# One high-weight product of 512 columns for both parts of h in the projection of an SSD recurrence, with the halves of the bank added on VectorE

## The chip, the cores and the metric

The kernel runs on one core of one Trainium2 chip. The metric is the device time of one execution in microseconds (us). Before the change three runs gave 1707.39, 1708.99 and 1709.05 us, median 1708.99. The profiled execution took 1709.76 us, of which the profile's span covers 1708.0 us.

## The reference

One decoder layer on x of 2048 tokens by 1024 features, all float32. `h` is a normalised and modulated x; `proj = h @ w_in` is split among a gated linear attention group (GLA) and a Mamba-2 group (SSD); both results are joined, multiplied by `w_out`, normalised and added to x. The change lies in the SSD part, cut here to what it computes:

```
z, xbc, dt_raw = parts of h @ w_in
xbc = silu(causal_depthwise_conv(xbc, conv_w, conv_b))      # 4 taps per channel, plus a bias
xs, B, C = split(xbc)
dt = softplus(dt_raw + dt_bias);  A = -exp(a_log)
y = ssd_chunked(xs, dt, A, B, C)     # h_t = exp(dt_t A) h_{t-1} + dt_t B_t x_t^T, y_t = C_t h_t
y = y + d_skip * xs;  y = rms_norm(y * silu(z)) per group
```

Every product with a weight is made to nearly full float32 precision out of three products: with w = w_hi + w_lo and h = h_hi + h_lo (hi is the part that the fast format keeps, lo the rest), w·h is taken as w_hi·h_hi + w_hi·h_lo + w_lo·h_hi.

## The kernel before, in words

The kernel has three stages: `front` (norms, GLA, most of the projection), `ssd` (the SSD recurrence with its own part of the projection) and `project_out`. The change touches `ssd` alone, which begins at about 786 us of the span.

`ssd` goes over 2 groups of heads, and in each over 8 blocks of 256 tokens: 16 **steps**. A step projects the block n in eight **units** and, between them, works off the recurrence of the block before, n-1, in two **tiles** of 128 tokens:

- Units 0 to 5 (`u < UZ`) are convolved channels. A unit is 8 slices of the contraction (KT) times 3 products (PASSES), so 24 matmuls with a weight slice of 128x128 as the stationary operand and 256 token columns moving (L1805). All accumulate in the left half of one bank of PSUM, `ps[:, PROJ + u % 2, 0:B2]`.
- Units 6 and 7 are the gate z: 24 matmuls of 512 columns each (L1809).

Each engine goes through the units in an order written out by hand, and a unit waits for the one two before it to have left its bank (`unit_out`).

- **PE** (`tensor`): tile_in of tile 0 (transposes, L1833 and L1836, and one product, L1837); units 0, 1; tile_out of tile 0 (L1845, L1852, L1857); tile_in of tile 1; units 2, 3; tile_out of tile 1; units 4, 5; turn of tile 0 (L1865); units 6, 7; turn of tile 1.
- **ACT** (`scalar`): evacuates each unit. For units 0 to 5 that is a copy of the bank's left half to `before` (L1550) and, of the same columns, times the last tap plus the bias, to `acc` (L1552). Between them stand the high parts of the next h (L1542), the squares (L1576) and normed rows (L1583) of both tiles, one SiLU over all six units (L1562), then after unit 6 the table load and exponentials of `decays` (L1567, L1568), which wait for `seg_ready`, the evacuation of z (L1557) and the rows y (L1593).
- **DVE** (`vector`): tile_in (L1704 to L1713), the three other taps of each unit (L1684, three instructions, each waiting for the one before by `conv_step`), the low parts of h (L1668), tile_out (L1724, L1727, L1731, L1735), the history of three columns (L1697) and last the 16 instructions of `segments` (L1745), behind which `seg_ready` comes.
- **POOL** (`gpsimd`): per tile `ends` (L1473), `decay_state` (L1480) and `skip` (L1488); after both tiles the small steps to 1/rms (L1494, L1497) and y_diff (L1509).
- **SP** and the DMA queues load h, weights and store y; the change does not touch them.

The waits that matter below: PE's product L1852 waits for DVE's L1713 (`wt_ready`); PE's turn L1865 waits for ACT's L1583 (`yn_ready`), that one for POOL's L1497, which stands on POOL behind `skip` of tile 1, which waits for DVE's L1724 of tile 1. `seg_ready` leads to ACT's exponentials, behind which ACT evacuates z and then unit 0 of the next step.

Of the kernel before, what the change touches and what calls it, by code (L numbers as in the profile page):

```python
# [21 lines left out]
ALU = mybir.AluOpType  # L22
ACT = mybir.ActivationFunctionType

P = 128
HI, LO = 0, 1

PASSES = ((HI, HI), (HI, LO), (LO, HI))
# [3 lines left out]
def wait(eng, sem, count):  # L32

    if not isinstance(count, int) or count > 0:
        eng.wait_ge(sem, count)
# [1262 lines left out]
def ssd(nc, sems, y_stored, unit_done, h_ready, xd_ready, w_rows, w_sum_d, conv_col, convb_col, d_row, norm_col, ps, ident, tok, w, w_raw, hl_all, halves, w_even,  # L1298
        h_d, ac_d, y_d, column, T, KT, G, HG, GW, XT, NS, SP_, INNER, VAL, TAPS, B2, TB2):

    UB, UC, UX, UZ = 0, 1, 2, 2 + XT
    UCONV, U = UZ, UZ + XT
# [3 lines left out]
    HIST = TAPS - 1  # L1306

    PROJ, X, BC, Y, YI, ST, YT = 0, 2, 3, 4, 5, 6, 7
# [5 lines left out]
    with ExitStack() as ctx:  # L1314
        def sb(name, shape, dt=F32):
            return ctx.enter_context(nc.sbuf_tensor(name, shape, dt))

        def sem(name):
            return sems.enter_context(nc.semaphore(name))

        hl = hl_all[:, 0].rearrange("p k c n -> p (k c n)").rearrange("p (q k c n) -> p q k c n", q=2, k=KT, c=2)
# [3 lines left out]
        before = sb("c_before", [P, UCONV, HIST + B2])  # L1325
        acc = sb("c_acc", [P, UCONV, B2])
# [29 lines left out]
        conv_step = sem("c_conv_step"); conv_ready = sem("c_conv_ready")  # L1356
# [20 lines left out]
        def order(g, u):  # L1377

            return u - UZ if g == 0 else g * U - UZ + u
# [5 lines left out]
        def channel(g, u):  # L1385

            return INNER // P + (u - UB) * G + g if u < UX else g * XT + u - UX
# [128 lines left out]
        def scalar(act):  # L1516
# [27 lines left out]
            def evacuate(n, g, u, par):  # L1544
                act.wait_ge(unit_done, n * UP + u + 1)
                if u < UCONV:

                    wait(act, hist_ready, n)
                    ch = channel(g, u)
                    act.activation(before[:, u, HIST:], ps[:, PROJ + u % 2, 0:B2], ACT.Copy)  # L1550
                    wait(act, xbc_ready, n)
                    act.activation(acc[:, u, :], ps[:, PROJ + u % 2, 0:B2], ACT.Identity,  # L1552
                                   scale=conv_col[:, HIST, ch:ch + 1], bias=convb_col[:, ch:ch + 1]
                                   ).then_inc(unit_out, 1)
                else:
                    wait(act, gated_ready, (n - 1) * TB2)
                    act.activation(z[:, par, u - UZ, :], ps[:, PROJ + u % 2, :], ACT.Silu).then_inc(unit_out, 1)  # L1557
# [91 lines left out]
        def vector(dve):  # L1649
# [29 lines left out]
            def convolve(n, g, u):  # L1679

                dve.wait_ge(unit_out, n * UP + u + 1)
                ch = channel(g, u)
                for k in range(HIST):
                    op = dve.scalar_tensor_tensor(out=acc[:, u, :], in0=before[:, u, k:k + B2],  # L1684
                                                  scalar=conv_col[:, k, ch:ch + 1], in1=acc[:, u, :],
                                                  op0=ALU.mult, op1=ALU.add)
                    if k < HIST - 1:
                        op.then_inc(conv_step, 1)
                        dve.wait_ge(conv_step, (n * UCONV + u) * (HIST - 1) + k + 1)
                op.then_inc(conv_ready, 1)  # L1690

            def history(n, s_last):
# [100 lines left out]
        def tensor(pe):  # L1793

            def unit(n, g, u, par):

                if g > 0 or u >= UZ:
                    pe.wait_ge(w_ready, order(g, u if u < UZ else U - 1) + 1)
                wait(pe, unit_out, n * UP + u - 1)
                for k in range(KT):  # L1800
                    if u == 0 and k % QK == 0 and not (isinstance(n, int) and n < 2):
                        pe.wait_ge(h_ready, (n - 2) * QS + k // QK + 1)
                    for i, (a, b) in enumerate(PASSES):
                        if u < UZ:
                            mm = pe.matmul(ps[:, PROJ + u % 2, 0:B2], w[:, u, k, a, :], hl[:, par, k, b, :],  # L1805
                                           start=(k == 0 and i == 0), stop=(k == KT - 1 and i == 2))
                        else:
                            t = u - UZ
                            mm = pe.matmul(ps[:, PROJ + u % 2, :], hl[:, par, k, a, t * P:(t + 1) * P],  # L1809
                                           w_z[:, k, b, :], start=(k == 0 and i == 0),  # L1810
                                           stop=(k == KT - 1 and i == 2))
                mm.then_inc(unit_done, 1)
# [402 lines left out]
```

## Time and profile before

| | before |
|---|---|
| median of 3 runs | 1708.99 us |
| profiled execution, its span | 1709.76 us, 1708.0 us |
| PE busy (matmuls) | 1625.9 us, 95% |
| weight loads busy | 1400.2 us, 82% |
| DVE busy | 1053.3 us, 62% |
| ACT busy | 841.4 us, 49% |
| POOL busy | 388.7 us, 23% |
| L1805, 2304 matmuls of 256 columns | 295.3 us busy |
| L1684, 288 instructions of the taps | 161.5 us busy |
| L1550 and L1552, 96 each | 36.9 and 53.9 us busy |

How to read it: busy shares are of the whole span, over three stages with different limits. A matmul's own duration overlaps that of the next one, so the pace of a run of matmuls is read from the starts of two groups in the timeline and not from a mean duration. "Idle before, releaser" names the instruction whose semaphore ended the wait; in the timeline a row with xN merges N instructions that follow each other on the line.

### The profile page before, as it was taken

What the parts mean: (1) busy time and instruction counts of PE and PEld (TensorE: products, weight loads), DVE (VectorE), ACT (ScalarE), POOL (GpSimd) and SP (SyncE); (2) the same over time, 40 slices, a digit from 0 to 9 for tenths busy, and PEclk for the clock granted to TensorE, in tenths of its full rate; (3) what the DMA queues carried; (4) which work ended last, traced back from release to release, by engine and by line L of the source; (5) the groups of instructions that cost most, each with busy time, mean ns of one, the idle gap of its engine ahead of it and who ended that gap; (6) DMA issues with size and microseconds to landing.
All of it is one profiled execution on the core that took longest, in us unless ns stands there. A gap on an engine that the chain in (4) does not pass through costs nothing. (4 is left out here: it accounts for less than half of the span.)

```text
span 1708.0 us, 27489 instructions
## 1 busy us (share of the span) xinstructions
PE 1625.9 (95%) x10022; PEld 1400.2 (82%) x10022; DVE 1053.3 (62%) x1752; ACT 841.4 (49%) x1496; POOL 388.7 (23%) x449
## 2 busy tenths in 40 slices
PE   5899999999899999998999999999999999999996
PEld 5688888888788888877888887888888878888885
DVE  3543554465544554445677777876777754785986
ACT  5555555545544554453554545655544545234332
POOL 5000000110422222200232222222322220451421
PEclk9899999999999999998999999999999999999998
DMA  9423252255333533344132124322222226675885
GB/s 279 164 87 112 83 178 71 72 167 145 126 117 127 189 125 130 127 125 136 50 112 75 68 74 142 117 81 78 103 74 74 99 87 221 233 241 169 302 273 181
DMA packets 131359, 231.16 MB, mean 135 GB/s; under 512 B 9907, under 2 KB 81859, under 8 KB 126134
## 3 DMA queue, kind: packets, MB, share of 16 engines
q1 hardware_dynamic: 121830, 189.71, 34.6%
q10 hardware_dynamic: 8592, 39.85, 6.4%
q0 software_dynamic: 832, 0.22, 0.2%
q8 instruction: 63, 1.03, 0.2%
q14 instruction: 42, 0.34, 0.1%
HBM read 177.05 MB, written 52.70 MB: 135 GB/s over the span
## 5 line engine op out<-in xcount | busy, mean ns | idle before, releaser
L1131 PE MATMUL ps<-hl,w 128*128 128x512 f32 x1488 | 374.1, 400 | 0.1
L1131 PEld LDWEIGHTS ps<-hl,w 128*128 128x128 f32 x1488 | 274.9, 189 | 56.6 <-issue 1.4
L1805 PE MATMUL ps<-hl,w 128*128 128x256 f32 x2304 | 295.3, 288 | 5.0 <-PEq L302 5.0
L1805 PEld LDWEIGHTS ps<-hl,w 128*128 128x128 f32 x2304 | 283.1, 193 | 13.2 <-issue 13.1
L1137 PE MATMUL ps<-w,hl 128*128 128x256 f32 x1536 | 203.1, 289 | 3.8 <-DVE w L830 3.8
L1137 PEld LDWEIGHTS ps<-w,hl 128*128 128x128 f32 x1536 | 192.8, 193 | 6.5 <-DVE w L830 4.2
L1684 DVE SCALAR_TENSOR_TENSOR c_acc<-c_before,conv_col,c_acc 128x256 f32<-128x256 f32 x288 | 161.5, 562 | 46.5 <-ACT c_acc L1552 39.5
L1809 PE MATMUL ps<-hl 128*128 128x512 f32 x768 | 178.6, 391 | 0.0
L1809 PEld LDWEIGHTS ps<-hl 128*128 128x128 f32 x768 | 143.0, 188 | 29.3 <-DVE hl L1653 0.2
L2188 PE MATMUL ps<-w,hl 128*128 128x512 f32 x720 | 164.2, 389 | 0.4 <-DVE hl L2127 0.4
L2188 PEld LDWEIGHTS ps<-w,hl 128*128 128x128 f32 x720 | 135.0, 188 | 28.8 <-issue 0.8
L1550 ACT ACTIVATE c_before<-ps 128x256 f32<-128x256 f32 x96 | 36.9, 384 | 220.6 <-PE ps L1805 220.6
L454 POOL TENSOR_SCALAR mse<-ms 128x1 f32<-128x1 f32 x60 | 15.6, 260 | 567.1 <-ACT squares L629 567.1
L2188 PE MATMUL ps<-hl 128*128 128x512 f32 x576 | 131.0, 389 | 0.0
L2188 PEld LDWEIGHTS ps<-hl 128*128 128x128 f32 x576 | 108.1, 188 | 22.4
L819 DVE TENSOR_TENSOR hl<-x_sb,hl 128x1024 fp32r<-128x1024 f32 x48 | 60.1, 1253 | 57.5 <-ACT hl L613 57.4
L880 DVE SCALAR_TENSOR_TENSOR state<-state,dec,ps 128x256 f32<-128x256 f32 x56 | 26.9, 480 | 105.4 <-PE ps L1174 105.3
L830 DVE TENSOR_TENSOR w<-w_raw,w 128x1024 fp32r<-128x1024 f32 x30 | 37.4, 1251 | 55.3 <-ACT w L559 55.3
L1488 POOL TENSOR_TENSOR c_yi<-c_yi,c_xd 128x512 f32<-128x512 f32 x32 | 41.4, 1293 | 131.9 <-DVE c_yi L1724 131.9
L890 DVE SCALAR_TENSOR_TENSOR y<-ps,norm_col,gz 128x128 f32<-128x128 f32 x120 | 36.3, 343 | 56.8 <-PE ps L1182 33.2
L2147 DVE TENSOR_TENSOR d_mixed<-d_mixed,ps 128x512 f32<-128x512 f32 x64 | 42.4, 683 | 44.6 <-PE ps L2188 23.6
L1745 DVE SCALAR_TENSOR_TENSOR c_decay<-c_ac,tok,c_past 128x128 f32<-128x128 f32 x256 | 68.6, 345 | 0.0
(247 smaller groups left out, 2624.8 us busy)
## 6 DMA issues: line engine op xcount, KB each, us to landing
x_sb<-h SPq DMA_DIRECT2D x52, 512.0 KB, 3.9
w_raw<-in_w_in SPq DMA_DIRECT2D x42, 512.0 KB, 4.4
c_ac<-step_sums ACTq DMA_DIRECT2D x16, 1024.0 KB, 4.7
d_a_raw<-mixed_in SPq DMA_DIRECT2D x29, 512.0 KB, 4.0
c_h_raw<-h SPq DMA_DIRECT2D x56, 256.0 KB, 2.8
d_a_raw<-mixed_in SPq DMA_DIRECT2D x11, 1024.0 KB, 5.6
w_sums<-late ACTq DMA_DIRECT2D x8, 1280.0 KB
w_raw<-w_sums SPq DMA_DIRECT2D x40, 256.0 KB, 3.9
```

Of the source, the lines that this page charges most:

```text
L819: last = dve.tensor_tensor(hl[:, n % 2, ks, LO, :], raw, hl[:, n % 2, ks, HI, :].bitcast(F32), ALU.subtract)
L830: dve.tensor_tensor(lo, w_raw[:, u % 2], hi.bitcast(F32), ALU.subtract).then_inc(w_ready, 1)
L1131: mm = pe.matmul(ps[:, PROJ + u % 2, :], w[:, u, k, a, :], hl[:, par, k, b, :], start=(k == 0 and i == 0), stop=(k == KT - 1 and i == 2))
L1137: mm = pe.matmul(ps[:, PROJ + u % 2, half * DV:(half + 1) * DV], hl[:, par, k, a, t * P:(t + 1) * P], w_v[:, k, b, :], start=(k == 0 and i ...
L1488: pool.tensor_tensor(yi[:, :, :], yi[:, :, :], xd[:, :, :], ALU.add).then_inc(skip_ready, 1)
L1550: act.activation(before[:, u, HIST:], ps[:, PROJ + u % 2, 0:B2], ACT.Copy)
L1684: op = dve.scalar_tensor_tensor(out=acc[:, u, :], in0=before[:, u, k:k + B2], scalar=conv_col[:, k, ch:ch + 1], in1=acc[:, u, :], op0=ALU. ...
L1745: last = dve.scalar_tensor_tensor(out=decay[:, h, t * P:(t + 1) * P], in0=ac[:, h, t * P:(t + 1) * P], scalar=own, in1=past[:, :], op0=ALU ...
L1805: mm = pe.matmul(ps[:, PROJ + u % 2, 0:B2], w[:, u, k, a, :], hl[:, par, k, b, :], start=(k == 0 and i == 0), stop=(k == KT - 1 and i == 2))
L1809: mm = pe.matmul(ps[:, PROJ + u % 2, :], hl[:, par, k, a, t * P:(t + 1) * P], w_z[:, k, b, :], start=(k == 0 and i == 0), stop=(k == KT - ...
L2147: last = dve.tensor_tensor(mixed[:, p, r, c, :], old, bank, ALU.add if how > 0 else ALU.subtract)
L2188: mm = pe.matmul(ps[:, j % 8, :], halves[:, j % 4, k, a, :], weight(i)[:, k, b, :], start=(k == 0 and q == 0), stop=(k == KT - 1 and q == 2))
```

## The change

Per unit 0 to 5 and slice k, the two products with the high part of the weight become one: w_hi stays in the array and h_hi and h_lo, which lie side by side in `hl`, move as 512 columns into the whole bank. The left half then holds w_hi·h_hi + w_lo·h_hi and the right half w_hi·h_lo. ACT copies both halves out, the right one to `acc`; DVE adds them into `before` and takes the last tap and the bias, in two more instructions per unit.

```diff
@@ evacuate (ACT)
-                    ch = channel(g, u)
                     act.activation(before[:, u, HIST:], ps[:, PROJ + u % 2, 0:B2], ACT.Copy)
                     wait(act, xbc_ready, n)
-                    act.activation(acc[:, u, :], ps[:, PROJ + u % 2, 0:B2], ACT.Identity,
-                                   scale=conv_col[:, HIST, ch:ch + 1], bias=convb_col[:, ch:ch + 1]
-                                   ).then_inc(unit_out, 1)
+                    act.activation(acc[:, u, :], ps[:, PROJ + u % 2, B2:2 * B2], ACT.Copy).then_inc(unit_out, 1)
@@ convolve (DVE)
                 ch = channel(g, u)
+                steps = (n * UCONV + u) * (HIST + 1)
+                dve.tensor_tensor(before[:, u, HIST:], before[:, u, HIST:], acc[:, u, :], ALU.add).then_inc(conv_step, 1)
+                dve.wait_ge(conv_step, steps + 1)
+                dve.tensor_scalar(acc[:, u, :], before[:, u, HIST:], conv_col[:, HIST, ch:ch + 1],
+                                  convb_col[:, ch:ch + 1], ALU.mult, ALU.add).then_inc(conv_step, 1)
+                dve.wait_ge(conv_step, steps + 2)
                 for k in range(HIST):
...
-                        dve.wait_ge(conv_step, (n * UCONV + u) * (HIST - 1) + k + 1)
+                        dve.wait_ge(conv_step, steps + k + 3)
@@ unit (PE)
-                    for i, (a, b) in enumerate(PASSES):
-                        if u < UZ:
-                            mm = pe.matmul(ps[:, PROJ + u % 2, 0:B2], w[:, u, k, a, :], hl[:, par, k, b, :],
-                                           start=(k == 0 and i == 0), stop=(k == KT - 1 and i == 2))
+                    if u < UZ:
+                        both = hl[:, par, k].rearrange("p c n -> p (c n)")
+                        if k == 0:
+                            pe.matmul(ps[:, PROJ + u % 2, :], w[:, u, k, HI, :], both, start=True, stop=False)
+                        mm = pe.matmul(ps[:, PROJ + u % 2, 0:B2], w[:, u, k, LO, :], hl[:, par, k, HI, :],
+                                       start=False, stop=False)
+                        if k > 0:
+                            mm = pe.matmul(ps[:, PROJ + u % 2, :], w[:, u, k, HI, :], both, start=False,
+                                           stop=(k == KT - 1))
```

On PE, unit 2 of a step, where the unit waits for its bank. Before:

```order
L1805 MATMUL ps<-hl,w 128x256 [waits c_unit_out]
L1805 MATMUL ps<-hl,w 128x256 x23
```

and with the change, the start of the same unit:

```order
L1809 MATMUL ps<-hl,w 128x512 [waits c_unit_out]
L1810 MATMUL ps<-hl,w 128x256 x2
L1813 MATMUL ps<-hl,w 128x512
L1810 MATMUL ps<-hl,w 128x256
L1813 MATMUL ps<-hl,w 128x512
```

A unit has 16 matmuls in place of 24, 8 of 512 columns and 8 of 256, over as many columns in all; the same wait stands ahead of the first.

On DVE, tile_in of tile 0 and units 0 and 1 up to tile_out of tile 0. Before:

```order
L1713 COPY c_btok<-ps 128x128
L1684 SCALAR_TENSOR_TENSOR c_acc<-c_before,conv_col,c_acc 128x256 [waits c_unit_out]
L1684 SCALAR_TENSOR_TENSOR c_acc<-c_before,conv_col,c_acc 128x256 [waits c_conv_step] x2
L1684 SCALAR_TENSOR_TENSOR c_acc<-c_before,conv_col,c_acc 128x256 [waits c_unit_out]
L1684 SCALAR_TENSOR_TENSOR c_acc<-c_before,conv_col,c_acc 128x256 [waits c_conv_step] x2
L1668 TENSOR_TENSOR hl<-c_h_raw,hl 128x2x256 [waits c_h_hi]
L1724 TENSOR_TENSOR c_yi<-ps,tok 128x512 [waits c_yi_done]
```

and with the change:

```order
L1716 COPY c_btok<-ps 128x128
L1681 TENSOR_TENSOR c_before<-c_before,c_acc 128x256 [waits c_unit_out]
L1683 TENSOR_SCALAR c_acc<-c_before,conv_col,convb_col 128x256 [waits c_conv_step]
L1687 SCALAR_TENSOR_TENSOR c_acc<-c_before,conv_col,c_acc 128x256 [waits c_conv_step] x3
L1681 TENSOR_TENSOR c_before<-c_before,c_acc 128x256 [waits c_unit_out]
L1683 TENSOR_SCALAR c_acc<-c_before,conv_col,convb_col 128x256 [waits c_conv_step]
L1687 SCALAR_TENSOR_TENSOR c_acc<-c_before,conv_col,c_acc 128x256 [waits c_conv_step] x3
L1665 TENSOR_TENSOR hl<-c_h_raw,hl 128x2x256 [waits c_h_hi]
L1727 TENSOR_TENSOR c_yi<-ps,tok 128x512 [waits c_yi_done]
```

A unit has five instructions in place of three, each waiting for the one before it. Nothing changes its place. ACT, POOL and SP issue as many instructions as before, in the same order.

## Rows read from the trace of the kernel before

**Rows 1.** Busy time by stretch; columns PE, PEld, DVE, ACT, POOL, PEclk, DMA share, GB/s.

```profile
900.00:1000.00 100.00, 100.00 (x767) 87.53 (x766) 73.59 (x154) 51.69 (x100) 27.87 (x30) 1.00 0.20 69
```

**Rows 2.** Timeline of PE, 900 to 940 us; columns start, us, engine, instruction.

```profile
900.05 0.39 PE L1837 MATMUL ps<-c_xbc 128*128 128x128 f32 x2
900.19 5.99 PE L1805 MATMUL ps<-hl,w 128*128 128x256 f32 x48
906.02 1.02 PE L1845 MATMUL ps<-c_state,c_xbc 128*128 128x512 f32 x2
...
914.77 0.60 PE L1865 MATMUL ps<-ident,c_yn 128*128 128x128 f32 x4
915.12 11.16 PE L1809 MATMUL ps<-hl 128*128 128x512 f32 x48
926.12 0.60 PE L1865 MATMUL ps<-ident,c_yn 128*128 128x128 f32 x4
...
927.10 0.39 PE L1837 MATMUL ps<-c_xbc 128*128 128x128 f32 x2
...
936.62 0.39 PE L1837 MATMUL ps<-c_xbc 128*128 128x128 f32 x2
```

**Rows 3.** Timeline of DVE, 900 to 940 us.

```profile
909.57 0.68 DVE L1724 TENSOR_TENSOR c_yi<-ps,tok 128x512 f32<-128x512 f32 x1
...
915.84 1.53 DVE L1684 SCALAR_TENSOR_TENSOR c_acc<-c_before,conv_col,c_acc 128x256 f32<-128x256 f32 x3 [0.61 <-ACT c_acc L1552]
...
918.11 4.29 DVE L1745 SCALAR_TENSOR_TENSOR c_decay<-c_ac,tok,c_past 128x128 f32<-128x128 f32 x16
...
931.27 4.41 DVE L1684 SCALAR_TENSOR_TENSOR c_acc<-c_before,conv_col,c_acc 128x256 f32<-128x256 f32 x6 [1.36 <-ACT c_acc L1552]
```

**Rows 4.** Timeline of ACT, 900 to 940 us.

```profile
913.34 0.72 ACT L1583 ACTIVATE c_yn<-c_yt,c_rstd 128x512 f32<-128x512 f32 x1
...
924.43 0.23 ACT L1567 ACTIVATE c_chunk<-c_ac 128x16 f32<-128x16 f32 x1
...
928.92 1.14 ACT L1593 ACTIVATE c_y<-ps,ssd_norm_col 128x128 f32<-128x128 f32 x4
930.40 0.39 ACT L1550 ACTIVATE c_before<-ps 128x256 f32<-128x256 f32 x1 [0.34 <-PE ps L1805]
930.68 0.56 ACT L1552 ACTIVATE c_acc<-ps,convb_col,conv_col 128x256 f32<-128x256 f32 x1
```

**Rows 5.** Durations of three DVE instructions elsewhere: min/median/max in ns, by line.

```profile
L961 DVE TENSOR_TENSOR late<-late x1: 425/425/425, 314.6 to 314.6; 128x256 f32<-128x256 f32 x1
L953 DVE TENSOR_SCALAR late<-late,a_neg x1: 356/356/356, 313.4 to 313.4; 128x256 f32<-128x256 f32 x1
L791 DVE TENSOR_SCALAR first_full<-first_full,gain,mod x4: 541/544/546, 35.0 to 55.9; 128x512 f32<-128x512 f32 x4
```

**Rows 6.** Timeline of DVE, 934.20 to 934.25 us: one tap by itself.

```profile
934.16 0.48 DVE L1684 SCALAR_TENSOR_TENSOR c_acc<-c_before,conv_col,c_acc 128x256 f32<-128x256 f32 x1
```

**Rows 7.** Timeline of POOL, 900 to 940 us.

```profile
912.08 0.57 POOL L1497 TENSOR_TENSOR c_rstd<-c_mse,c_neg_half 128x1 f32<-128x1 f32 x1
...
931.47 1.23 POOL L1473 TENSOR_TENSOR c_xend<-c_xdt,tok 128x512 f32<-128x512 f32 x1
```

**Rows 8.** Timeline of PE, 1050 to 1125 us, around the change of groups.

```profile
1057.59 1.98 PE L1852 MATMUL ps<-c_xdt,c_decay 128*64 128x64 f32 x32 [3.72 <-DVE c_btok L1713]
...
1080.75 0.39 PE L1837 MATMUL ps<-c_xbc 128*128 128x128 f32 x2
...
1098.43 1.15 PE L1852 MATMUL ps<-c_xdt,c_decay 128*64 128x64 f32 x32 [1.17 <-DVE c_btok L1713]
...
1108.13 0.66 PE L1865 MATMUL ps<-ident,c_yn 128*128 128x128 f32 x4 [1.74 <-ACT c_yn L1583]
...
1120.51 0.39 PE L1837 MATMUL ps<-c_xbc 128*128 128x128 f32 x2
```

**Rows 9.** Timeline of DVE, 1060 to 1125 us: one of the low parts of a weight.

```profile
1099.93 1.22 DVE L1653 TENSOR_TENSOR hl<-w_raw,hl 128x1024 fp32r<-128x1024 f32 x1
```

More of the change, by code:

```diff
@@ L1802, in unit @@
                         pe.wait_ge(h_ready, (n - 2) * QS + k // QK + 1)
-                    for i, (a, b) in enumerate(PASSES):
-                        if u < UZ:
-                            mm = pe.matmul(ps[:, PROJ + u % 2, 0:B2], w[:, u, k, a, :], hl[:, par, k, b, :],
-                                           start=(k == 0 and i == 0), stop=(k == KT - 1 and i == 2))
-                        else:
-                            t = u - UZ
+                    if u < UZ:
[7 more added lines that the diff above has]
+                                           stop=(k == KT - 1))
+                    else:
+                        t = u - UZ
+                        for i, (a, b) in enumerate(PASSES):
                             mm = pe.matmul(ps[:, PROJ + u % 2, :], hl[:, par, k, a, t * P:(t + 1) * P],
```

## The prediction

> **What bounds the kernel now.** I read three views: the busy times by stretch, then the timeline of each engine over one step, then the waits around the change of groups. In the stretches of the SSD stage PE is busy 100% and DVE 74% [rows 1], so PE is the bound there, but DVE is no small second. In PE's timeline the same product comes back after 936.62 - 900.05 = 36.57 us [rows 2]; that is one step, and PE shows no wait in it. The starts of tile_in repeat so in 12 of the 16 steps. The step at the end of group 0 takes what 1080.75 - 927.10 leaves beside three of 36.57, 43.9 us, and the next one 1120.51 - 1080.75 = 39.76 us [rows 2, 8]. In these two DVE also makes low parts of weights, and PE waits for DVE. So the stage has two chains close to each other: PE's own 36.57 us, and a loop through DVE and ACT that PE hides as long as it is shorter. I work out that loop.
>
> **The loop, before.** Its DVE part goes from the first tap of unit 0 to the end of `segments`. The first begins at 931.27, the last ends one step after 918.11 + 4.29, at 958.97 [rows 3]: 27.70 us. DVE is idle in it for 0.61 us behind ACT [rows 3], which a late DVE would not be, so 27.09 are left. They hold waits for POOL's `skip` that stay. ACT's part begins with the exponentials at 924.43, which may not start before `seg_ready`, and goes through z and y to 928.92 + 1.14 = 930.06 [rows 4]: 5.63 us. Then unit 0 is evacuated and its taps begin: 930.40 to 931.27, 0.87 us [rows 3, 4]. Sum 33.6 us, 3 us less than PE's step.
>
> **PE's part of the change.** 48 products of 256 columns take 906.02 - 900.19 = 5.83 us, 121.5 ns each; 48 of 512 columns take 926.12 - 915.12 = 11.00 us, 229.2 ns each [rows 2]. Three of 256 were 364.5 ns; one of each is 350.7. That saves 13.8 ns per slice, 0.11 us per unit, 0.66 per step, and over 768 slices (96 units by 8) 10.6 us. That is all that PE can give, for the columns stay as many. PE alone would need 35.9 us per step. The gain is bounded by nothing (if the mixed run keeps today's pace) and by 768 times a whole weight's turn; nothing in the rows speaks for more than the difference of the two paces. The Trainium skill (TensorE: Matmul & The Clock Gate, Back-to-back issue gap) puts the fixed part of a matmul at some 2.5 ns beside its columns, by which leaving out 768 would give 2 us; the trace has 121.5 and 229.2 where that rule has about 109 and 216, so the fixed part here is larger and I keep 10.6.
>
> **ACT's part.** The second evacuation, 0.56 us, becomes a copy like the first, 0.39 [rows 4]: 0.17 us less per unit. In the loop it counts once per step, for unit 0; elsewhere ACT is ahead of DVE.
>
> **DVE's part.** Two instructions per unit, neither of them in the trace in this form. The add has the shape of L961: 425 ns. The multiply-add with two column scalars lies between L953 (356 ns, 256 wide, one column scalar) and L791 (544 ns, 512 wide, two) [rows 5]; I take 410. Each is followed by a wait for itself, and of such a chain the rows show the price: three taps in 1.53 us, the last 0.48, so one begins each 0.52, 0.03 to 0.04 us after the end of the one before [rows 3, 6]. Together 0.455 + 0.44 = 0.90 us per unit, 5.4 per step. Lowest by the rows: 425 + 356 with the gaps, 0.84. Highest: both like a tap, 1.04.
>
> **The loop, after.** 33.6 - 0.17 + 5.4 = 38.8 us. It is now the longer chain: +2.3 us per step (38.5 to 39.7 by the two ends). Nothing covers the 5.4 us. The cover was DVE's idle time, and the loop had only 3 us of it.
>
> What one sees on PE follows from it. L1724 of tile 1 stands behind the taps of units 0 to 3. Units 1, 2 and 3 lie in one unbroken piece, 2.7 us more. Today 1/rms is there at 912.08 + 0.57 = 912.65, the normed rows could be at 913.4, and PE comes to its turn at 914.77 [rows 2, 4, 7]: 1.4 us of room. PE comes 0.4 us sooner, so it waits some 1.5 us there, and some 1 us at L1852. The trace has done this experiment once: in the step from 1080.75, DVE has one low part of a weight more in each of four units, 1.22 us each [rows 9], and PE waits 1.17 us at L1852 and 1.74 at L1865, 2.9 in all [rows 8], as much as the step is longer than 36.57. With up to 4.9 us more on DVE the step became 3.2 us longer; 2.3 net for 5.4 more on DVE, 1.0 less on ACT and 0.66 less on PE is in line.
>
> **POOL's hold on DVE.** Units 0 and 1 take 4.41 us together with no gap to ACT inside, where two units like the one at 915.84 would take 3.06 [rows 3]; the 1.35 us more lie where POOL works on L1473 and, right behind it, L1480 [rows 7]. So VectorE's taps and these instructions hold each other up. This is in the 27.70 us already. After the change POOL's y_diff, which follows ACT's late rows y, may fall on unit 0 too and hold one more instruction, about 0.6 us per step. I leave that out of the sum and keep it for the upper end. The Trainium skill (SBUF — State Buffer, Who interferes with whom) says that a VectorE instruction with two SBUF inputs, and a multiply-add from SBUF to SBUF, shares a lock with GpSimd; the trace agrees for the taps, and by the page both new instructions can be held too.
>
> **The sum.** 11 steps of 36.57 at +2.3: 25 us. The first step of each run of them, starting with room: +0.5. The step of 39.76 us has no room left: +5.4. The step of 43.9 waits partly for weights to land: +3. The last step, with its own low parts of weights, and the tail behind it: +3. The first step has no tile work, so it gains 0.7. Together +36 us on the profiled 1709.76, which stands 0.8 us above the median: 1745 us.
>
> **The rivals.**
>
> - *DVE hides it (faster).* If the loop stayed under 35.9 us, PE's saving would come out whole: 1709 - 10.6 = 1698 us. It needs a pair of at most (35.9 - 33.4) / 6 = 0.41 us, against 0.78 for the bare durations of the nearest rows. For it: DVE is only 74% busy [rows 1]. Against it: most of its idle time lies between `segments` and the next tile_in, while ACT works through its own part of the loop, and DVE can't use it: tile_in needs PE's transposes. 7%.
> - *The bare trade (nearly the same).* The pair at about 0.5 us gives a loop of 36.4 to 36.6, within 0.2% of before. 3%.
> - *The holds fall away.* If the later POOL instructions meet DVE at work out of PSUM, the loop loses up to 1.3 us: 37.5 to 38 per step, +1 to +1.4, in all +15 to +22: 1724 to 1731 us. 17%.
> - *The cheap price.* The Trainium skill (VectorE: DVE Perf Modes, the section on the TRN2 errata) has 58 cycles plus the elements, halved for a multiply-add: 327 and 194 ns. As a mechanism of this kernel: a pair of 0.52 and its gaps, 0.58 us, so 36.9 us per step, +4 on the 11 steps and +5 to +7 at the change of groups, 1720 us. L961 has 425 where that rule has 327, so 5%, taken with the case above.
> - *Forecast.* The loop at 38.4 to 39.7 us, 1735 to 1758 us. 58%.
> - *Dearer.* One more hold per step (+8 us), or both new instructions at a tap's price or held (+10 or more): 1758 to 1768. Or PE's waits grow together until the clock falls: after the wait of 3.72 us the products at L1852 took 1.98 us in place of 1.15 [rows 8], and the next stretch was slower for some 3 us. Once in every step that would be 1780. My waits of 1 and 1.5 us lie apart, and after 1.17 and 1.74 L1852 kept its 1.15 us. 10%.
>
> **How the numbers follow.** The likeliest case gives 1745 us. The range of 1722 to 1764 takes in the forecast, most of the case without holds, and the next hold; it leaves out the faster and the same case (10%), the low end of the cheap price and the case of the clock. A measurement of this kernel can tell about 0.2%, 3.4 us, from no change. Faster by more: 7%; within: 3%; slower: 90%.
>
> **What would show each step right or wrong.** In the profile after: steps of about 38.9 us between two tile_ins in the middle of a group; 512 and 256 columns at a pace of 351 ns per pair (a unit pair in 5.6 us, not 5.83); the add at 0.42 to 0.46 and the multiply-add at 0.36 to 0.45 us; five instructions of an undisturbed unit in about 2.4 us; waits of PE at L1865 for ACT's c_yn and at L1852 for c_btok that were not there; DVE's idle time at the first L1704 of a step about halved, and ACT's wait before the evacuation of unit 0 gone. The forecast is wrong if PE stays without waits, if the pair costs under 0.5 us, or if the PE pace of the mixed run is worse than today's, which the loop would hide but the profile would show.

## The result, and the profile after

The changed kernel took 1764.5 us (median of 4 runs, 1761.98 to 1765.28) against 1709.0 for the kernel before on the same chip: 1.0328 times as long, 95% interval 1.0316 to 1.0341. The profiled execution's span grew from 1708.0 to 1762.5 us, by 54.5. The forecast was 1745 us, +36 on the profiled execution, with a range of 1722 to 1764: the sign and the place were right, but the median lies 19.5 us above the forecast and 0.5 us above the range. Between the two spans the loss is some 18 us larger than forecast.

Busy times on the page of the changed kernel:

```profile
PE 1631.3 (93%) x9254; PEld 1361.7 (77%) x9254; DVE 1141.3 (65%) x1944; ACT 821.8 (47%) x1496; POOL 383.1 (22%) x449
...
L1687 DVE SCALAR_TENSOR_TENSOR c_acc<-c_before,conv_col,c_acc 128x256 f32<-128x256 f32 x288 | 148.9, 517 | 10.2
...
L1681 DVE TENSOR_TENSOR c_before<-c_before,c_acc 128x256 f32<-128x256 f32 x96 | 52.8, 550 | 39.2 <-ACT c_acc L1551 39.2
```

PE has 768 matmuls fewer, DVE 192 instructions more. In the stretch that stood at 100% PE and 74% DVE [rows 1] PE is no longer full (columns: PE, PEld, DVE, ACT, POOL, PEclk, DMA share, GB/s):

```profile
900.00:1000.00 100.00, 90.23 (x614) 71.41 (x613) 82.05 (x163) 39.05 (x85) 27.06 (x28) 1.00 0.20 69
```

PE's waits inside the SSD stage, 786 to 1450 us (waited for, us in total, times, longest). Before, the first of these rows was 6.6 us in 3 waits, the second 2.0 us in 2, the third absent:

```profile
PE ps L1861 <- DVE c_btok L1716: 29.0, 15, 3.7
PE ps L1874 <- ACT c_yn L1580: 20.2, 13, 2.6
PE ps L1809 <- ACT c_z L1554: 5.9, 9, 1.2
```

The length of each step is the distance between two starts of the last transpose of tile 0's tile_in (L1836 before, L1845 after; "PE's step" below). In us, with the start of the first:

```
         first    steps ->
before   817.28   36.56 36.58 36.57 36.57 36.58 36.57 43.93 39.76 36.57 36.57 36.58 36.57 36.57 36.58 37.02
after    818.38   37.52 38.96 40.69 40.68 40.65 40.46 46.00 45.59 38.80 39.03 40.79 40.72 40.69 40.50 42.29
```

Leaving out the first and the last step and the two at the change of groups, there are eleven middle steps, of two kinds. Three are 38.8 to 39.0 us, as forecast (38.8). Eight are 40.5 to 40.8. These eight are the ones for which ACT's program is a loop (`act.Fori`); the first two and the last two steps of a group are written out. ACT's timeline tells them apart. ACT loads a table (`ACT_TABLE_LOAD`, 1.28 us) ahead of the exponentials of `decays`. In a loop step:

```profile
933.42 1.28 ACT L1564 ACT_TABLE_LOAD   x1 [1.48 <-DVE c_decay L1748]
934.72 0.23 ACT L1564 ACTIVATE c_chunk<-c_ac 128x16 f32<-128x16 f32 x1
934.85 1.90 ACT L1565 ACTIVATE c_decay<-c_decay 128x2048 f32<-128x2048 f32 x1
...
939.21 1.14 ACT L1590 ACTIVATE c_y<-ps,ssd_norm_col 128x128 f32<-128x128 f32 x4
...
940.48 0.42 ACT L1551 ACTIVATE c_acc<-ps 128x256 f32<-128x256 f32 x1
```

and in a step that is written out:

```profile
1100.88 1.28 ACT L1564 ACT_TABLE_LOAD   x1
1103.31 0.23 ACT L1564 ACTIVATE c_chunk<-c_ac 128x16 f32<-128x16 f32 x1 [1.14 <-DVE c_decay L1748]
```

In the loop the table load waits for DVE's `segments` and only then takes its 1.28 us; written out, it runs while DVE still works. The lists of the program's instructions say why: in both the load stands right ahead of `c_chunk`, but another wait stands ahead of the load. In the source `decays` waits first for `seg_ready`, then for `decayed_ready`. Written out, the first wait rides on `c_chunk` and the second on the load:

```
L1564 ACT_TABLE_LOAD [waits c_decayed_ready]
L1564 ACTIVATE c_chunk<-c_ac 128x16 [waits c_seg_ready]
```

In the loop, where both counts come from a register, the second one rides on `c_chunk` and the first is an instruction of its own ahead of the load:

```
L1564 ACT_TABLE_LOAD
L1564 ACTIVATE c_chunk<-c_ac 128x16 [waits c_decayed_ready]
```

The other half of the loop, DVE in the same step (the `segments` before it, unit 0, unit 1, and the `segments` at its end), and POOL beside it:

```profile
929.04 4.28 DVE L1748 SCALAR_TENSOR_TENSOR c_decay<-c_ac,tok,c_past 128x128 f32<-128x128 f32 x16
...
940.93 1.15 DVE L1681 TENSOR_TENSOR c_before<-c_before,c_acc 128x256 f32<-128x256 f32 x1 [2.45 <-ACT c_acc L1551]
942.11 1.01 DVE L1683 TENSOR_SCALAR c_acc<-c_before,conv_col,convb_col 128x256 f32<-128x256 f32 x1
943.16 2.20 DVE L1687 SCALAR_TENSOR_TENSOR c_acc<-c_before,conv_col,c_acc 128x256 f32<-128x256 f32 x3
945.28 0.42 DVE L1681 TENSOR_TENSOR c_before<-c_before,c_acc 128x256 f32<-128x256 f32 x1
945.73 0.41 DVE L1683 TENSOR_SCALAR c_acc<-c_before,conv_col,convb_col 128x256 f32<-128x256 f32 x1
946.18 1.52 DVE L1687 SCALAR_TENSOR_TENSOR c_acc<-c_before,conv_col,c_acc 128x256 f32<-128x256 f32 x3
947.62 0.68 DVE L1665 TENSOR_TENSOR hl<-c_h_raw,hl 128x512 fp32r<-128x512 f32 x1
...
969.72 4.29 DVE L1748 SCALAR_TENSOR_TENSOR c_decay<-c_ac,tok,c_past 128x128 f32<-128x128 f32 x16
```

```profile
940.51 1.29 POOL L1509 TENSOR_TENSOR c_y_diff<-c_y 128x512 f32<-128x512 f32 x1 [14.12 <-ACT c_y L1590]
941.75 1.22 POOL L1473 TENSOR_TENSOR c_xend<-c_xdt,tok 128x512 f32<-128x512 f32 x1
942.94 1.10 POOL L1480 TENSOR_TENSOR c_decayed<-c_state,c_chunk 128x512 f32<-128x512 f32 x1
```

Add and multiply-add run at 0.42 and 0.41 us where nothing holds them; unit 1 takes 947.62 - 945.28 = 2.34 us up to the start of what follows. Unit 0 takes 945.28 - 940.93 = 4.35, while `y_diff`, `ends` and `decay_state` of POOL run beside it one after another; an experiment below moves them.

The loop can be closed from these rows. DVE's part runs from 940.93 to 969.72 + 4.29 = 974.01, 33.08 us. The `segments` before ended at 929.04 + 4.28 = 933.32. The load brings ACT to 934.72, 1.40 us; from the first exponential to the end of y (939.21 + 1.14 = 940.35) are 5.63; then 0.58 to DVE's add. Together 33.08 + 1.40 + 5.63 + 0.58 = 40.69, the length of the step.

### The profile page after: what moved, and what is told of

It is laid out like the page before. It is cut to its first block and busy times, and to the rows that moved or that the text cites. A ratio compares the mean times of both kernels' runs of the same rounds, so it can differ in the third digit from the quotient of the medians.

```text
span 1762.5 us, 26241 instructions
## 1 busy us (share of the span) xinstructions
PE 1631.3 (93%) x9254; PEld 1361.7 (77%) x9254; DVE 1141.3 (65%) x1944; ACT 821.8 (47%) x1496; POOL 383.1 (22%) x449
## 5 line engine op out<-in xcount | busy, mean ns | idle before, releaser
L1131 PE MATMUL ps<-hl,w 128*128 128x512 f32 x1488 | 374.5, 401 | 0.1
L1131 PEld LDWEIGHTS ps<-hl,w 128*128 128x128 f32 x1488 | 275.1, 189 | 56.7 <-issue 1.4
L1813 PE MATMUL ps<-hl,w 128*128 128x512 f32 x672 | 243.0, 400 | 0.0
L1810 PE MATMUL ps<-hl,w 128*128 128x256 f32 x768 | 201.3, 283 | 0.0
L1810 PEld LDWEIGHTS ps<-hl,w 128*128 128x128 f32 x768 | 147.9, 193 | 10.8 <-issue 4.7
L1687 DVE SCALAR_TENSOR_TENSOR c_acc<-c_before,conv_col,c_acc 128x256 f32<-128x256 f32 x288 | 148.9, 517 | 10.2
L1813 PEld LDWEIGHTS ps<-hl,w 128*128 128x128 f32 x672 | 128.2, 191 | 26.6
L1681 DVE TENSOR_TENSOR c_before<-c_before,c_acc 128x256 f32<-128x256 f32 x96 | 52.8, 550 | 39.2 <-ACT c_acc L1551 39.2
L1861 PEld LDWEIGHTS ps<-c_xdt,c_decay 128*64 128x64 f32 x1024 | 34.0, 143 | 54.3 <-DVE c_btok L1716 42.9
```

The costliest lines, as they stand in the source:

```text
L1131: mm = pe.matmul(ps[:, PROJ + u % 2, :], w[:, u, k, a, :], hl[:, par, k, b, :], start=(k == 0 and i == 0), stop=(k == KT - 1 and i == 2))
L1681: dve.tensor_tensor(before[:, u, HIST:], before[:, u, HIST:], acc[:, u, :], ALU.add).then_inc(conv_step, 1)
L1810: mm = pe.matmul(ps[:, PROJ + u % 2, 0:B2], w[:, u, k, LO, :], hl[:, par, k, HI, :], start=False, stop=False)
L1813: mm = pe.matmul(ps[:, PROJ + u % 2, :], w[:, u, k, HI, :], both, start=False, stop=(k == KT - 1))
L1861: mm = pe.matmul(ps[i * CH:(i + 1) * CH, Y, h * SP_:(h + 1) * SP_], decay[:, h, t * P + i * CH:t * P + (i + 1) * CH], xdt[:, h, :], start= ...
```

## The experiments

All kernels were timed beside the kernel before on the same chip; the factor is the time over that of before, with its 95% interval. Times in us.

**Is it the wait ahead of the table load?** In the loop steps alone the two waits of `decays` change places, so that the one for `seg_ready` rides on `c_chunk`.

```diff
             def decays(n):
+                if not isinstance(n, int):
+                    wait(act, decayed_ready, n * TB2)
                 act.wait_ge(seg_ready, n + 1)
-                wait(act, decayed_ready, n * TB2)
+                if isinstance(n, int):
+                    wait(act, decayed_ready, n * TB2)
```

In the changed kernel:

> The changed kernel, with the two waits of decays on ACT exchanged inside the loops over steps, so that the table load no longer stands behind the wait for seg_ready there (8 of 16 steps). Theory (the DVE/ACT loop sets the step, and in these 8 steps the table load of 1.28 us lies in it): steps of 40.7 us fall to 38.8 to 39.2, total 1764.5 - 8 x 1.5 to 1.8 = 1750 to 1753 us. Rival (the excess over my 38.8 comes from POOL holding DVE up more often): the load is off the path, no change, 1764.

In the kernel before:

> The same exchange of waits in the kernel before. Theory (PE sets the step there, the loop has 3 us of room): no change, 1709 within 0.2%, steps 36.57 us. Rival (the load already cost something before): 1700 or less.

Measured: 1751.4 (1.0249, 1.0232 to 1.0266) and 1706.8 (0.9993, 0.9983 to 1.0002). The eight loop steps fell from 40.7 to 39.3, the other three stayed at 38.8 to 39.0. ACT in a loop step of the changed kernel with the exchanged waits, and `segments` on DVE, whose last 13 instructions end at 931.23:

```profile
929.87 1.28 ACT L1567 ACT_TABLE_LOAD   x1
931.26 0.23 ACT L1567 ACTIVATE c_chunk<-c_ac 128x16 f32<-128x16 f32 x1
```

```profile
927.73 3.50 DVE L1751 SCALAR_TENSOR_TENSOR c_decay<-c_ac,tok,c_past 128x128 f32<-128x128 f32 x13
```

The load is off the path: 13 us of the loss. In the kernel before the same exchange changes nothing, since there PE sets the step. The experiments below that say so are built on the changed kernel with exchanged waits.

**Which half of the change costs?** First PE's products alone, in the kernel before; ACT and DVE work as before on the left half of the bank, so the product w_hi·h_lo is left out of the result.

```diff
@@ the kernel before, unit (PE): the products as in the change
@@ evacuate (ACT), convolve (DVE): as before
```

> Only the products of the change: one of 512 and one of 256 columns per slice; ACT and DVE as before, the right half of the bank (w_hi times h_lo) is computed and left out of the result. Theory: PE is the bound, steps 36.57 - 0.66 = 35.9 us, total 1709 - 10.6 = 1698 to 1700 us. Rival (a mixed run of matmuls has no gain, or the 2.5 ns of the page): 1707 to 1709.

Then the ACT and DVE part alone, with PE's products as before; ACT copies the left half twice and DVE adds the copies, so the convolution works on twice its input.

```diff
-                    act.activation(acc[:, u, :], ps[:, PROJ + u % 2, 0:B2], ACT.Identity,
-                                   scale=conv_col[:, HIST, ch:ch + 1], bias=convb_col[:, ch:ch + 1]
-                                   ).then_inc(unit_out, 1)
+                    act.activation(acc[:, u, :], ps[:, PROJ + u % 2, 0:B2], ACT.Copy).then_inc(unit_out, 1)
@@ convolve (DVE): the five instructions of the change
```

> Only DVE's and ACT's part: the three products of 256 columns as before, ACT copies the left half twice, DVE adds and multiplies in the two new instructions (the convolution then works on twice its input). Theory: the loop does not hold PE's products, so the time is that of the change itself, 1764 +- 4 us, although PE has 10.6 us more to do. Rival (PE's waits add to its own work): 1764 + 10 = 1775.

Measured: PE alone 1702.7 (0.9965, 0.9951 to 0.9979), a gain of 5 to 6 us where 9 to 11 were expected. Its middle steps are 36.12, so a step saves 0.45 and not 0.66. And one step, the one after the change of groups, became longer, 41.43 instead of 39.76. PE's timeline there:

```profile
1092.78 1.15 PE L1858 MATMUL ps<-c_xdt,c_decay 128*64 128x64 f32 x32 [1.50 <-DVE c_btok L1713]
...
1102.46 0.66 PE L1871 MATMUL ps<-ident,c_yn 128*128 128x128 f32 x4 [1.87 <-ACT c_yn L1583]
1102.87 12.80 PE L1815 MATMUL ps<-hl 128*128 128x512 f32 x48
1115.52 0.60 PE L1871 MATMUL ps<-ident,c_yn 128*128 128x128 f32 x4
```

The 48 products of 512 columns take 1115.52 - 1102.87 = 12.65 us where they took 11.00 [rows 2]. The granted clock over them is 0.88 (PEclk, third figure from the end), so the engine was for a part of them at the lower of its two levels, 1.2 instead of 2.4 GHz; it was 1.00 over the same work of the kernel before, in the second fence:

```profile
1102.00:1116.00 14.00, 13.54 (x57) 11.07 (x58) 9.00 (x27) 9.31 (x16) 1.05 (x2) 0.88 0.13 37
```

```profile
1108.00:1122.00 14.00, 13.87 (x74) 11.93 (x75) 10.05 (x29) 10.65 (x18) 1.04 (x2) 1.00 0.20 55
```

Before, the waits ahead of it were 1.17 and 1.74 us [rows 8]; now they are 1.50 and 1.87. The step is accounted for: 39.76 - 0.45 + 0.46 more of waits + 1.65 = 41.42. Why the clock fell is open. Longer waits alone don't explain it, for in the middle steps of the changed kernel's first group PE waits 1.95 and 1.49 us at the same two places, and the clock stays at 1.00 (the row of 900 to 1000 us above):

```profile
913.96 1.15 PE L1861 MATMUL ps<-c_xdt,c_decay 128*64 128x64 f32 x32 [1.95 <-DVE c_btok L1716]
...
923.27 0.66 PE L1874 MATMUL ps<-ident,c_yn 128*128 128x128 f32 x4 [1.49 <-ACT c_yn L1580]
```

The ACT and DVE part alone: 1761.9 (1.0315, 1.0298 to 1.0333), with loop steps of 40.7. That is the whole loss of the change within 3 us. PE's saving is invisible in it: PE's products don't lie in the loop.

**What does one DVE instruction cost?** On the version with exchanged waits, the multiply-add is issued twice in each unit; the counts of `conv_step` grow with it.

```diff
@@ convolve (DVE), behind the multiply-add
+                dve.tensor_scalar(acc[:, u, :], before[:, u, HIST:], conv_col[:, HIST, ch:ch + 1],
+                                  convb_col[:, ch:ch + 1], ALU.mult, ALU.add).then_inc(conv_step, 1)
+                dve.wait_ge(conv_step, steps + 3)
...
```

> The changed kernel with the exchanged waits and the new multiply-add issued twice per unit (same result): the suspected cost doubled. Theory (DVE's instructions of all six units lie one for one in the loop): 0.445 x 6 = 2.7 us more per step, over 15 steps and the tail +40 to +43, 1791 to 1795 us. Rival (PE's wait at the turn sets the step, with only the units 0 to 3 ahead of it): 4 x 0.445 = 1.8 per step, +27, 1778.

Measured: 1795.9 (1.0518, 1.0501 to 1.0536), 1 us above the expected range; loop steps 41.96, 2.63 longer: six times 0.44. DVE's own work lies on the path in full.

**Does POOL's y_diff hold DVE?** On the version with exchanged waits, POOL does y_diff of a step after `ends` and `decay_state` of the next step's tile 0.

```diff
                     decay_state(r, g, t)
+                    if t == 0 and not (g == 0 and isinstance(b, int)):
+                        difference(r - 1)
                     skip(r, t)
                 for t in range(TB2):
                     rstd_of(r, t)
+
+            def difference(r):
                 pool.wait_ge(y_ready, r * TB2 + TB2)
                 wait(pool, y_stored, r * 32)
...
+            difference(G * S - 1)
```

> The changed kernel with the exchanged waits (1751 us, middle steps 39.3 us), and POOL's y_diff moved from the end of a step to behind the first two POOL instructions of the next, so that these two run while DVE reads PSUM in tile_in, and not while it works on unit 0. Theory (POOL's instructions hold DVE up inside the loop, 2 us in unit 0: its five instructions take 4.35 us where undisturbed ones take 2.35): steps shorter by 1.3 to 2 us, 1751 - 15 x 1.3 to 2 = 1721 to 1732 us. Rival (DVE waits at unit 0 for ACT anyway, so the holds are free): 1751.

The same move in the kernel before:

> The kernel before with y_diff moved in the same way: control. Theory (PE sets the step): middle steps stay at 36.57 us, only the two steps around the change of groups may gain a little: 1706 to 1709 us.

Measured: 1737.6 (1.0179, 1.0162 to 1.0196) and 1706.4 (0.9995, 0.9985 to 1.0004). A step became 1.2 us shorter, not the 2 us that all holds together would be, and the time stayed almost 6 us above the expected range. POOL and DVE in a loop step of the changed kernel so altered:

```profile
969.23 1.04 POOL L1473 TENSOR_TENSOR c_xend<-c_xdt,tok 128x512 f32<-128x512 f32 x1 [10.36 <-DVE c_xdt L1715]
970.23 1.05 POOL L1480 TENSOR_TENSOR c_decayed<-c_state,c_chunk 128x512 f32<-128x512 f32 x1
971.62 1.30 POOL L1513 TENSOR_TENSOR c_y_diff<-c_y 128x512 f32<-128x512 f32 x1 [0.34 <-ACT c_y L1598]
```

```profile
972.08 1.12 DVE L1689 TENSOR_TENSOR c_before<-c_before,c_acc 128x256 f32<-128x256 f32 x1 [1.12 <-ACT c_acc L1556]
973.23 0.41 DVE L1691 TENSOR_SCALAR c_acc<-c_before,conv_col,convb_col 128x256 f32<-128x256 f32 x1
```

`ends` and `decay_state` now run beside DVE's work out of PSUM and hold nobody, but y_diff waits for ACT's last y and starts 0.46 us ahead of the first add, which it holds (1.12 instead of 0.42). Two of the three holds are gone, one stays. In the kernel before the same move gave nothing in the middle steps, where PE sets the step.

**Is PE's wait at the turn on the path?** On the version with exchanged waits, POOL computes tile 0's 1/rms before skip of tile 1.

```diff
                     decay_state(r, g, t)
+                    if t == 1:
+                        rstd_of(r, 0)
                     skip(r, t)
-                for t in range(TB2):
-                    rstd_of(r, t)
+                rstd_of(r, 1)
```

> The kernel with the change and the exchanged waits in the loops (1751 us) in which POOL works out tile 0's 1/rms before it does skip of tile 1, not behind it. The normed rows then come earlier and PE's wait at the turn of tile 0 for c_yn (1.5 us in the middle steps, 23.8 us in all) should go or fall under 0.3 us. Theory: that wait is a symptom, PE waits out there the slack that the loop through DVE and ACT gives it, and loses it elsewhere (at the z units for c_z, or at c_btok): middle steps stay at 39.3 us, time 1748 to 1753. Rival: the turn is on the path that sets the step: steps of 37.8 to 38.0, time 1728 to 1733.

Measured: 1751.8 (1.0265, 1.025 to 1.028), with loop steps of 39.3 as before the move, but for one pair (40.9 and 37.5). In the first of the pair the granted clock fell for a part of the step; the two together are 78.4 us, as long as two others, so the loop took no notice of it:

```profile
985.00:999.00 14.00, 12.07 (x81) 9.24 (x80) 11.60 (x22) 4.12 (x11) 5.50 (x6) 0.88 0.12 37
```

The turn's wait fell from 23.8 us to 2.0. Of these 21.8 us, 14.6 came back at the two places in the first rows below, which had 25.1 and 1.2 us, and most of the rest at shorter ones. PE's waits with the move:

```profile
PE ps L1865 <- DVE c_btok L1720: 30.2, 15, 3.7
PE ps L1813 <- ACT c_z L1555: 10.7, 13, 1.2
...
PE ps L1878 <- ACT c_yn L1584: 2.0, 1, 2.0
```

As long as the loop through DVE and ACT sets the step, PE waits out its slack wherever the order lets it; which wait shows it says nothing about its cost.

**Can the idea be made to pay?** The last tap and the bias can leave DVE: with the taps divided by the last one, DVE adds the halves and does three taps (four instructions), and ACT's SiLU, now one per unit, takes the last tap as its scale and the bias. This needs last taps that are not zero. Beside it: exchanged waits, y_diff moved, and one low part of h moved behind `segments`.

```diff
-                dve.tensor_scalar(acc[:, u, :], before[:, u, HIST:], conv_col[:, HIST, ch:ch + 1],
-                                  convb_col[:, ch:ch + 1], ALU.mult, ALU.add).then_inc(conv_step, 1)
...
-                                                  scalar=conv_col[:, k, ch:ch + 1], in1=acc[:, u, :],
+                                                  scalar=ratio[:, k, ch:ch + 1],
+                                                  in1=before[:, u, HIST:] if k == 0 else acc[:, u, :],
...
-                act.activation(xbc[:, par], acc[:, :, :], ACT.Silu).then_inc(xbc_ready, 1)
+                ch = channel(g, u)
+                op = act.activation(xbc[:, par, u], acc[:, u, :], ACT.Silu, scale=conv_col[:, HIST, ch:ch + 1],
+                                    bias=convb_col[:, ch:ch + 1])
```

> A version meant to keep PE's saving: the changed kernel with the exchanged waits, y_diff late, the last low part of h behind the segments, and four DVE instructions per unit in place of five: the taps are divided by the last one once (three ratios per channel), the sum of the halves goes into the first tap directly, and the last tap and the bias become scale and bias of ACT's SiLU, which is taken per unit. Theory (loop = before + 6 x 0.455 - 1.4 of holds - 0.6 + some 1 us of SiLU): the loop falls to about 35 to 36 us, PE's 36.1 us bound again: 1703 to 1710 us. Rival (ACT's six SiLUs put it back): 1720 or more.

Measured: 1711.9 (1.0033, 1.0022 to 1.0044), with steps of 36.5 and a few microseconds lost at the change of groups and in the last step; somewhat above what was expected. Then the 1/rms move was added to it, and as a control all three moves were made in the kernel before:

> The version with four DVE instructions per unit (the last tap and the bias in ACT's SiLU), y_diff and one low part of h moved, the exchanged waits, 1711.9 us, and now tile 0's 1/rms before skip of tile 1. There the middle steps are 36.5 us, where PE alone needs 36.1, and PE still waits at the turn (5.9 us in all). Theory: with the loop at or below PE's own time the turn wait costs what it shows: middle steps 36.1 to 36.3 and 3 to 6 us less, 1706 to 1709 us, about the kernel before. Rival (the loop still sets the step): 1710 to 1713.

> Control: the kernel before with the same moves that need no change of the products (y_diff, one low part of h, tile 0's 1/rms before skip of tile 1). PE has no wait in its middle steps, so steps stay at 36.57 us; at the change of groups PE waits less at the turn: 1703 to 1708 us. If the moves alone bring the gain, this one equals or beats the version with four instructions; by the theory that one should be ahead in the middle steps by 0.3 to 0.45 us each and behind at the change of groups.

and the three moves with the change's five DVE instructions:

> The kernel with the change, the exchanged waits and all three moves (y_diff, one low part of h, tile 0's 1/rms before skip of tile 1), with the five DVE instructions per unit of the change; only the cut to four, with the last tap in ACT's SiLU, is left out. Theory: the loop through DVE and ACT sets the step. Of its 38.1 us with y_diff moved, the low part of h takes 0.6 out, the 1/rms nothing: middle steps 37.4 to 37.6, time 1727 to 1733 us. With a sixth DVE instruction the step was 2.63 us longer, so a fifth is worth as much and the cut to four brings it under PE's 36.1. Rival: the moves were what brought the version with four down to 1702 us, and the fifth instruction fits into DVE's idle time once they are made: steps of 36.1 to 36.6, 1702 to 1710 us.

Measured, with PE's steps:

```
                                time     factor (95%)              steps ->
four DVE instr., 3 moves        1702.4   0.9971 (0.9960, 0.9983)   36.11 36.08 36.08 36.08 36.08 36.08 45.56 36.96 37.06 36.08 x6
before with 3 moves             1705.0   0.9986 (0.9977, 0.9994)   36.56 36.57 36.58 36.57 36.57 36.58 43.54 36.58 36.58 36.57 ...
five DVE instr., 3 moves        1732.7   1.0152 (1.0134, 1.0170)   36.10 37.42 38.24 38.04 38.00 37.75 46.96 41.84 38.27 37.64 ...
```

With four instructions PE has no wait left in the middle of a group and steps at its own 36.08, 0.49 us under 36.57. With five it is at 38.0, where 37.4 to 37.6 was expected, so the cut from five to four, with ACT's SiLU per unit that belongs to it, is worth 30 us. The moves alone don't do it, and the low part of h brought 0.1 per step, not the expected 0.6. Here the wait at the turn, which cost nothing at 39.3, was real: with it gone the time was 9.5 us shorter, more than the 3 to 6 expected. Of these, 6.8 lie in the steps and 1.3 in an earlier start of the first step, which differs among runs anyway. PE in two steps of the fast version, and its waits in the whole stage:

```profile
934.48 0.27 PE L1868 MATMUL ps<-ident,c_xbc 128*128 128x128 f32 x1
...
970.56 0.27 PE L1868 MATMUL ps<-ident,c_xbc 128*128 128x128 f32 x1
```

```profile
PE ps L1884 <- DVE c_btok L1732: 4.9, 3, 3.7
...
PE ps L1897 <- ACT c_yn L1595: 2.1, 1, 2.1
```

It is 0.3% faster than the kernel before. Against the control, 2.6 us or 0.15%, it is likely ahead: the intervals of the two factors overlap, but both were measured beside each other on one chip, and its six runs (1701.1 to 1703.2) lie below ten of the control's twelve (1702.2 to 1706.5). Twelve steps are shorter by some 6 us in all; the change of groups (45.56 against 43.54), the two steps behind it and a start 2 us later, which differs among runs anyway, take 5 of them back. The other 1.6 us of the lead lie behind the last step's start and were not followed.

## Why the prediction was right, and where it failed

**The bound moved, as said.** A loop through DVE and ACT took PE's place and showed itself in PE's waits for c_btok and c_yn. DVE's part alone gave 1761.9, and doubling one DVE instruction lengthened the step by all of it.

**DVE's prices were right.** 0.42 and 0.41 us against 0.425 and 0.410. An undisturbed unit takes 2.42 us from its first start to its last end (945.28 to 946.18 + 1.52), against 1.53 + 0.90. So the cheap-price rival falls. By the Trainium skill (VectorE: DVE Perf Modes, The TRN2 errata), whose table has 58 cycles plus the columns over the speed-up of the mode, the multiply-add would be 0.19 us, an estimate; the row has more than twice that. The formula that the same section gives for a float32 add, (N + 151) / 0.96, makes 424 ns, and agrees with the row. What the rows contradict is the table's fixed part, not the halving: from 256 to 512 columns the multiply-add grows from 0.41 to 0.54 us (L791 in [rows 5]), 0.13, and the product of two tensors, which has the add's form, to 0.69 from the add's 0.42, 0.27:

```profile
L1735 DVE TENSOR_TENSOR c_yt<-c_yt,c_z x32: 691/692/696, 829.4 to 1394.6; 128x512 f32<-128x512 f32 x32
```

**"The loop, after: 38.8 us" held in three of eleven middle steps.** In the eight others the step that failed is the loop's term "ACT's part", which "begins with the exponentials at 924.43" and was put at 5.63 us. `segments` had ended at 922.40 [rows 3]. The 2.03 us between the two, 1.28 of them the table load, stood in no term of the sum, as if they were slack that a late DVE would use up. In the kernel before, the times couldn't decide it: ACT was late there because PE was, and came to the load 0.7 us after `segments` had ended:

```profile
920.87 0.60 ACT L1557 ACTIVATE c_z<-ps 128x512 f32<-128x512 f32 x1 [1.98 <-PE ps L1809]
...
923.13 1.28 ACT L1567 ACT_TABLE_LOAD   x1
```

The order of the instructions could have: the account of ACT ahead of the prediction has the table load among what waits for `seg_ready`. In the loop steps the load does start behind that wait and costs 1.4 us in each: 40.69 = 38.8 + 1.4 + 0.6, less 0.1. Exchanging the waits gave 13.1 us back and brought the time to 1751.4, inside the forecast's range.

That the three written-out steps came out at 38.8 to 39.0 is luck in part. In the one with 38.80, DVE's part is 32.5 us as in the sum, but POOL holds unit 0 for some 1.8 us, not for the 1.35 that the sum had from before: the add is held there too (0.90 us in the row), and so are the multiply-add and a tap. The rest of DVE's part was shorter by as much. ACT's part is 5.42, not 5.63, and the way to the first add 0.84, not 0.70:

```profile
1152.98 0.90 DVE L1681 TENSOR_TENSOR c_before<-c_before,c_acc 128x256 f32<-128x256 f32 x1 [1.23 <-ACT c_acc L1551]
```

**The 0.6 is the hold that the sum left out.** The prediction had it that POOL's y_diff "may fall on unit 0 too and hold one more instruction, about 0.6 us per step", and kept it for the upper end: it did fall there, in every loop step. Unit 0 lost 2.0 us to POOL where before units 0 and 1 lost 1.35. DVE's part measured 33.08 against 32.5. It belonged in the sum: y_diff follows ACT's last y, and so does unit 0's evacuation, so both come late together. With the load's 1.4 us it makes, but for 0.1, what a loop step missed by. The rival in which the holds fall away was wrong outright. The Trainium skill (SBUF — State Buffer, Who interferes with whom) has VectorE and GpSimd block each other on a shared pair of ports; the trace agrees for the add (1.15 us at a hold, 0.42 without) and for the multiply-add with two column scalars (1.01 against 0.41).

**PE's saving was smaller.** Two units of the changed kernel take 910.99 - 905.30 = 5.69 us, not 5.6 (before 5.83 [rows 2]); a step of PE alone saves 0.45 to 0.49, not 0.66.

```profile
905.30 0.48 PE L1809 MATMUL ps<-hl,w 128*128 128x512 f32 x1
...
910.99 1.02 PE L1854 MATMUL ps<-c_state,c_xbc 128*128 128x512 f32 x2
```

A pair of 512 and 256 columns thus takes 355.6 ns, where the two paces taken apart add to 350.7. While DVE's loop is the bound this changes nothing.

**The case of the clock came in part, and at no price in the middle steps.** Before, the granted clock was below 1.00 in one place of the SSD stage from 790 us on, at the wait of 3.72 us [rows 8]. With the change it was so in five, two of them in middle steps, 1244 to 1258 and 1285 to 1299 us, both at 0.88:

```profile
1244.00:1258.00 14.00, 12.11 (x81) 9.59 (x81) 12.60 (x25) 4.18 (x11) 4.76 (x6) 0.88 0.07 21
```

These two steps took 40.79 and 40.72 us, as long as the others: a slower PE stays hidden behind the loop. What the three falls at the change of groups and in the last step cost was not separated.

**The sum, term by term** (forecast, measured from the step lengths): written-out middle steps 6.9, 7.1. Loop steps 18.4, 32.6. First step 0.5, 1.0. The 43.9 step 3, 2.1. The 39.76 step 5.4, 5.8. Last step and tail 3, 4.9. Start -0.7, +1.1. Of the 18 us missed, 14.2 are the loop steps, 1.9 the end, 1.8 the start. The start differs by that much between runs whose code up to there is the same: 814.8 us in the kernel before with exchanged waits, 817.3 without. The 1.9 of the end was not followed further.

## What to carry to other kernels

- A chain that is hidden today has to be summed with everything on it at the moment it becomes the bound: a table load, a register wait, another engine's port. What the trace shows as covered is not free afterwards. Read the order of the instructions at the wait, in the loop and outside it.
- A wait on the engine that used to be the bound is a symptom. Removing the turn's wait gave nothing while DVE's loop set the step, and some 7 us in the steps once four instructions had brought the loop near PE's own time.
- Trading matmuls for vector instructions is a trade of 0.07 to 0.08 us per unit on PE against 0.9 on DVE. It pays only if the second engine has that room inside its loop, not in its busy share.

## What the runs showed of the hardware that was not expected

- In this program ACT's exponentials have two waits and a table load ahead of them. With counts from a register the first wait, for `seg_ready`, is an instruction of its own ahead of the load, which starts behind it: 1.28 us in the open. With constant counts the wait for `seg_ready` stands behind the load, which then runs ahead of it. The order is the program's; the chip did as it says.
- Mixed runs of 512 and 256 columns cost some 5 ns per pair more than the two uniform paces.
- With PE's products alone the granted clock read 0.88 over 14 us behind waits of 1.50 and 1.87 us: 1.65 us lost on 48 matmuls, a quarter of what the 768 fewer matmuls gave. Behind 1.17 and 1.74 us in the kernel before it had stayed at 1.00, but so it did behind 1.95 and 1.49 us in the changed kernel. The length of the waits doesn't tell it alone.
- A multiply-add with two column scalars took 0.41 us for 256 columns and 0.54 for 512, an add 0.42 and a product of two tensors of 512 columns 0.69: the multiply-add pays half as much per column, but has the larger fixed part.
